# Suffix sums spread over query rows by TensorE, a reordered DMA queue, other PSUM banks for the output transposes, and loop weight tiles gathered in DRAM

## Chip, cores and metric

One core of one Trainium2 chip. The metric is the device time of one launch in microseconds (us), the median of several runs.

## What is computed

One inference step of a two-layer decoder trunk, width 1024, 16 heads of 64, all in fp32. There are 512 new prompt tokens (one sequence) and 64 sample tokens (8 sequences of 8), so 576 rows. Layer A is a gated short convolution over all rows. Its output gives one set of keys, values and log forget gates. Layer B projects queries and a SiLU gate and attends. The sample rows also attend to 2048 past rows for each sequence, kept in pages of 128 rows.

```python
q, z = jnp.split(_rmsnorm(x, g) @ w_in, 2, axis=-1)
s = jnp.einsum('nqhd,nkhd->nhqk', q, k) * (HEAD_DIM ** -0.5)
s = s + (fq - fk)                 # F: cumulative sum of the log forget values, past included
p = jax.nn.softmax(jnp.where(kpos <= qpos, s, -inf), axis=-1)
out = x + (einsum(p, v) * silu(z)) @ w_out
# k_all, v_all, F_all: cache pages named by page_table, then the new sample rows
```

For the past, fk enters as the sum of the log forget values behind a row (the suffix sum), one number for each sequence, head and past row.

## The kernel before

The kernel is written for the engines directly: each engine has its own instruction list in a fixed order, and semaphores tie them together. SyncE (SP) issues nearly all DMAs, in the order written.

Every fp32 product with a weight is made of three fp32r products (high by high, low by high, high by low). So each weight tile [128, 8, 128] is loaded raw (`w_raw`, two slots), scaled by the norm gains on GpSimd (POOL, L529 and L552), rounded to its high part on ScalarE (ACT, L630 or L681), and its low part is subtracted on VectorE (DVE) or POOL (L914, L998, L561).

The stages:

- The mixer, up to 235 us: 8 turns of 4 weight tiles, 48 matmuls each (L1294).
- The output slabs of layer A, to 300 us: 4 slabs of 256 columns, 5 row tiles each (L1320). DVE adds each tile to the residual (L993, `out_tile`), and TensorE (PE) waits for that before it reuses a bank. At their start DVE makes the suffix sums `logf_sums` (L1001), POOL stores them to DRAM as fp32, and SP waits for the stores before it loads on.
- The queries, to 385 us: 8 tiles (`query`).
- The loop `heads(i)`, eight turns, to 845 us. Turn i does two heads of the prompt and all the past of sample sequence i.
- The output slabs of layer B.

A turn of the loop, in PE's order: the tile of values is projected (`project(0)`), its last eighth after a wait for 8 of the 16 key pages. Key pages are transposed by 32 x 32 blocks on DVE (`turn_keys`, L1068). Then come the first half of the past scores (`past_scores(0)`, L1451, into the four banks T0, T1, C0, C1), the tile of keys (`project(1)`), the other half of the scores, and the z tile (`project(2)`) in pieces between other work. In DVE's and ACT's order: DVE adds the suffix sums to the scores and takes the maximum (L1099, then three tiny instructions L1104 to L1106 that give the softmax bias, semaphore `b_nbs`). ACT takes the exponential (L777, `b_es`), PE transposes the probabilities (L1264), and ACT and DVE copy them out (L747, L1081). PE then goes through 16 value pages (L1558, `b_used` frees a page's slot in `page_ring`). Between them it does four blocks of the prompt attention: `block_scores(r)`, on DVE `block_max(r)` (L1124, and the tiny L1129 and L1130), on ACT `block_exp(r)`, on DVE `block_divide(r)` (L1138), on PE `block_turn(r)`, `block_out(r)`. The next turn's key pages go into the slots as they come free.

On the side, POOL makes the next weight tiles: scale the z tile, `low_b` of it, norm the keys (`b_normed`), scale the next values tile, `low_b` of it once ACT has rounded it (`high_b(KT + 3*i + 3, 0)`), scale the next keys tile, copy the queries, `low_b` of that tile (`high_b(KT + 3*i + 4, 1)`).

Of the kernel before, what the change touches and what calls it, by code (L numbers as in the profile page):

```python
# [23 lines left out]
F32 = mybir.dt.float32  # L24
# [7 lines left out]
P = 128  # L32
# [81 lines left out]
def build(nc, ctx, x_prompt, x_sample, state_conv, cache_k, cache_v, cache_logf, page_table,  # L114
# [70 lines left out]
    LS = place("sum_past", [P, NB])  # L185
    assert at["top"] <= nc.sbuf_usable_end, at["top"]
# [11 lines left out]
    CS = place("logf_sums", [P, H, PAGE], over=at["sample_scores"])  # L198
    STN = place("state_rows", [2 * NB, D], over=at["new_keys"])
# [32 lines left out]
    def sem(name):  # L232
# [30 lines left out]
    b_turned, b_scored, b_taken = sem("k_pages_turned"), sem("past_scored"), sem("past_scores_taken")  # L263
# [49 lines left out]
    def _(sp):  # L313
# [36 lines left out]
        mixer(KT - 1, True)  # L350

# [13 lines left out]
        sp.wait_ge(s_sfx_st, 16 * NB)  # L365
# [60 lines left out]
        for m in range(KT):  # L426
            r = 32 * (m % 4) + 16 * (m // 4)
            sp.dma_start(CK[r:r + 16, :],
                         f_dram[2 * m:2 * m + 2, SEQ:TOK].unsqueeze(1).to_broadcast([2, NQ, NS])).then_inc(s_ck, 16)
        for n in range(4, KT + 3):  # L430
# [3 lines left out]
            else:  # L434
                load_w(*((wkv, D), (wkv, 0), (wqz, KT * P))[n - KT], (0, 1, 1)[n - KT])
# [11 lines left out]
        def values(pages, i, last):  # L447
# [4 lines left out]
            if not last:  # L452
                sp.wait_ge(b_split, KT + 3 * i + 1)
                load_w(wkv, (i + 1 + KT) * P, 0)

            for n in range(NPG):
# [3 lines left out]
                if n == 7 and not last:  # L460
                    sp.wait_ge(b_split, KT + 3 * i + 3)
                    load_w(wkv, (i + 1) * P, 1)
# [1218 lines left out]
```

## Time and profile before

| | us |
|---|---|
| Median of 3 runs (925.36 to 931.59) | 925.96 |
| The profiled execution, its own time | 924.18 |
| Its span (first to last instruction) | 922.4 |
| PE busy | 837.3 (91%) |
| DVE busy | 545.6 (59%) |
| ACT busy | 342.4 (37%) |
| POOL busy | 217.3 (24%) |
| Data moved by DMA | 206.39 MB |

The span and its rows belong to the one profiled execution. 1.8 us of its time lie outside of the span. Busy times of engines overlap, so what ends last has to be read from the waits. A turn is named here by S, the start of its first half of past scores: 385.6 in turn 0, 624.0 in turn 4, 681.8 in turn 5, 797.4 in turn 7, the last.

### The profile page before, as it was taken

The page shows a single profiled execution, that of the slowest core. Times are in us where ns is not written, and L with a number is a line of the kernel's source. Part 1 is how long each engine was busy: PE and PEld are TensorE (multiplying, and loading weights), DVE is VectorE, ACT ScalarE, POOL GpSimd, SP SyncE. Part 2 cuts the span into 40 slices and gives each one's busy share as a digit, 9 for nine tenths or more (in the row PEclk, how much of TensorE's full clock was granted, in tenths as well). Part 3 has the DMA queues.
Part 4 walks back from the last instruction along what each step waited for, and adds up shares of the span by engine and source line. Part 5 has one row for each costly group of instructions (what it writes and reads, how often), then busy time and mean ns, then how long its engine had stood idle before and what let it go on. Part 6 is the DMA issues. An engine that isn't in the chain of part 4 may idle for free.

```text
span 922.4 us, 22692 instructions
## 1 busy us (share of the span) xinstructions
PE 837.3 (91%) x8516; PEld 701.5 (76%) x8516; DVE 545.6 (59%) x1039; ACT 342.4 (37%) x728; POOL 217.3 (24%) x130
## 2 busy tenths in 40 slices
PE   3799999999998999698988988889888998897998
PEld 3799999999998899474765756567566675664998
DVE  4745565454436523747758578586695866946642
ACT  4333333332204444335345352452533525245210
POOL 2244333323211022213221321413223132130000
PEclk9999999999999999899999999999999999998999
DMA  7232323322554653298999999999999999994212
GB/s 212 69 88 72 91 70 89 91 68 91 140 137 122 238 178 120 71 365 267 315 370 299 376 349 318 395 317 379 366 329 397 292 381 391 312 402 140 92 46 104
DMA packets 148451, 206.39 MB, mean 224 GB/s; under 512 B 10527, under 2 KB 93136, under 8 KB 147266
## 3 DMA queue, kind: packets, MB, share of 16 engines
q1 hardware_dynamic: 138802, 199.40, 65.1%
q10 hardware_dynamic: 9088, 4.46, 1.6%
q0 software_dynamic: 528, 2.10, 0.8%
q8 instruction: 20, 0.33, 0.1%
q14 instruction: 13, 0.11, 0.0%
HBM read 195.29 MB, written 10.63 MB: 223 GB/s over the span
## 4 chain that ended last, share of the span: by engine, by line
PE 68%; DVE 14%; SPq 7%; issue 5%; DMA 4%; ACT 1%; DVEq 0%; POOL 0%; ACTq 0%; POOLq 0%
PE psum L1294 37%; PE psum L1320 10%; PE psum L1451 7%; DVE page_ring L1068 5%; SPq L387 4%; PE psum L1264 4%; PE psum L1558 3%; DMA page_ring<-in_cache_k 2%; PE psum L1491 1%; PE psum L1513 1%; DVE probs_odd L1138 1%; DMA w_raw<-in_a_w_in 1%; DMA w_raw<-in_a_w_out 1%; DVE tiny L1129 1%; DVE probs L1124 1%
## 5 line engine op out<-in xcount | busy, mean ns | idle before, releaser
L1294 PE MATMUL psum<-xn_high,w_high 128*128 128x256 f32 x992 | 226.8, 310 | 19.8 <-DVE page_ring L1068 16.9
L1294 PE MATMUL psum<-xn_low,w_high 128*128 128x256 f32 x992 | 213.6, 297 | 0.0
L1294 PE MATMUL psum<-xn_high,w_low 128*128 128x256 f32 x992 | 213.5, 297 | 0.0
L1294 PEld LDWEIGHTS psum<-xn_high,w_high 128*128 128x128 f32 x992 | 165.8, 191 | 52.8 <-issue 29.6
L1294 PEld LDWEIGHTS psum<-xn_high,w_low 128*128 128x128 f32 x992 | 168.2, 190 | 0.0
L1294 PEld LDWEIGHTS psum<-xn_low,w_high 128*128 128x128 f32 x992 | 168.1, 190 | 0.0
L1068 DVE STREAM_TRANSPOSE page_ring<-page_ring 128x1024 f32<-128x1024 f32 x128 | 149.5, 1215 | 6.2 <-DMA page_ring<-in_cache_k 5.6
L552 POOL TENSOR_TENSOR w_raw<-w_raw,gains 128x1024 f32<-128x1024 f32 x32 | 60.7, 1898 | 224.7 <-DMA w_raw<-in_b_w_in 213.4
L914 DVE TENSOR_TENSOR w_low<-w_raw,w_high 128x1024 fp32r<-128x1024 f32 x32 | 50.4, 1576 | 77.4 <-ACT w_high L630 77.4
L561 POOL TENSOR_TENSOR w_low<-w_raw,w_high 128x1024 fp32r<-128x1024 f32 x22 | 52.4, 2380 | 131.4 <-ACT w_high L681 131.4
L529 POOL TENSOR_TENSOR w_raw<-w_raw,gains 128x1024 f32<-128x1024 f32 x30 | 61.9, 2063 | 86.9 <-DMA w_raw<-in_a_w_in 86.9
L1558 PE MATMUL psum<-page_ring,p_turned 128*32 128x256 f32 x1024 | 75.6, 390 | 0.0
L1451 PE MATMUL psum<-page_ring,q_current 32*32 32x512 f32 x2048 | 73.5, 614 | 0.0
L630 ACT ACTIVATE w_high<-w_raw 128x1024 fp32r<-128x1024 f32 x32 | 33.9, 1060 | 94.1 <-PE psum L1294 66.7
L1451 PEld LDWEIGHTS psum<-page_ring,q_current 32*32 32x32 f32 x2048 | 34.2, 104 | 27.4 <-issue 18.1
L681 ACT ACTIVATE w_high<-w_raw 128x1024 fp32r<-128x1024 f32 x30 | 31.7, 1056 | 60.4 <-POOL w_raw L552 51.2
L1558 PEld LDWEIGHTS psum<-page_ring,p_turned 128*32 128x32 f32 x1024 | 23.5, 108 | 20.9 <-issue 13.7
L732 ACT ACTIVATE q_current<-queries 32x64 f32 (+1 forms) x128 | 32.5, 254 | 3.9 <-DVE queries L1045 1.0
L1081 DVE COPY probs_t<-psum 128x512 f32<-128x512 f32 (+3 forms) x32 | 15.4, 482 | 27.5 <-PE psum L1264 27.3
L1096 DVE COPY ks_t<-k_t 128x64 f32 (+1 forms) x8 | 1.6, 196 | 50.5 <-PE psum L1451 50.5
L797 ACT ACTIVATE probs<-probs,tiny 128x512 f32<-128x512 f32 (+1 forms) x32 | 19.3, 604 | 25.4 <-DVE tiny L1130 24.4
L1264 PE MATMUL psum<-constants,sample_scores 128*128 128x128 f32 x128 | 18.6, 278 | 10.6 <-DVE p_turned L1081 8.6
(243 smaller groups left out, 1431.8 us busy)
## 6 DMA issues: line engine op xcount, KB each, us to landing
page_ring<-in_cache_k SPq DMA_DIRECT2D x256, 256.0 KB, 6.2
page_ring<-in_cache_v SPq DMA_DIRECT2D x128, 512.0 KB, 9.6
w_raw<-in_a_w_in SPq DMA_DIRECT2D x32, 512.0 KB, 4.0
sample_scores<-suffix_scratch SPq DMA_DIRECT2D x8, 1024.0 KB, 12.4
w_raw<-in_b_w_in SPq DMA_DIRECT2D x16, 512.0 KB, 6.0
w_raw<-in_kv_w SPq DMA_DIRECT2D x16, 512.0 KB, 8.9
w_raw<-in_a_w_out SPq DMA_DIRECT2D x4, 1024.0 KB, 4.8
f_broad<-f_scratch SPq DMA_DIRECT2D x8, 512.0 KB, 7.6
```

The lines of the kernel that those rows point to most:

```text
L387: sp.dma_start(ring[:, n, e * HALF_D:(e + 1) * HALF_D], src.rearrange("a p n -> (a p) n")).then_inc(b_page[n], 16)
L529: pool.tensor_tensor(WR[:, q % 2, :, :], WR[:, q % 2, :, :], gain(G_A), ALU.mult).then_inc(a_scaled, 1)
L552: pool.tensor_tensor(WR[:, slot, :, :], WR[:, slot, :, :], gain(g), ALU.mult).then_inc(b_scaled, 1)
L561: pool.tensor_tensor(WL[:, slot, :, :], WR[:, slot, :, :], WH[:, slot, :, :].bitcast(F32), ALU.subtract).then_inc(b_split, 1)
L630: act.activation(WH[:, slot, :, :], WR[:, slot, :, :], ACT.Copy).then_inc(a_high, 1)
L914: dve.tensor_tensor(WL[:, slot, :, :], WR[:, slot, :, :], WH[:, slot, :, :].bitcast(F32), ALU.subtract).then_inc(a_split, 1)
L1068: dve.transpose(ring[:, n, :], ring[:, n, :]).then_inc(b_turned, 1)
L1264: return pe.transpose(out, src, CT[0:r, C_ID:C_ID + r])
L1294: mm = pe.matmul(PS[:, bank + h, 0:c.stop - c.start], w[:, k, :], x[:, k, c], start=(k == 0 and n == 0), stop=(k == KT - 1 and n == 2))
L1320: mm = pe.matmul(PS[0:r, bank, 0:SLAB], x[:, k, toks(t)], wp[:, k, :], start=(k == 0 and p == 0), stop=(k == KT - 1 and p == 2))
L1451: mm = pe.matmul(PS[32 * j:32 * j + 32, T0 + g, :].rearrange("p (n k) -> p n k", k=32), QC[32 * g:32 * g + 32, j, 64 * h + 32 * a:64 * h + ...
L1558: mm = pe.matmul(PS[32 * j:32 * j + 32, OS, 0:4 * HD].rearrange("p (a n) -> p a n", a=2), PTS[:, k, 32 * j:32 * j + 32], ring[:, k, :].rea ...
```

## The change

- The suffix sums are stored as three bf16 parts (ACT rounds, DVE subtracts, twice over). In a turn 48 rows of 4 KB are loaded instead of 128 rows of 8 KB. 16 bf16 matmuls with a 0/1 matrix `EACH` write them into the four score banks before the scores are added (`start=False`). DVE no longer adds; it takes one maximum over all four banks, and ACT takes the exponential from PSUM.
- The transposes of new keys and values go to the banks OP and OS. Those of the keys move ahead of the second half of the scores, those of the values right behind it. Four of the eight z pieces follow at once, then a wait for two of the exponentials ahead of `block_scores(0)`.
- `high_b(KT + 3*i + 3, 0)` moves on ACT from behind the probabilities' copies to just behind the values' copy, ahead of the exponentials. `high_b(KT + 3*i + 4, 1)` moves from after block 3 to between blocks 0 and 2.
- On DVE `block_divide(0)` goes ahead of `block_max(1)`, and `block_divide(3)` ahead of the first `turn_keys` of the next turn. Four key pages of turn 0 are transposed during the last two queries.
- The stores of new keys and values go from ACT's queue to SP's. SP reads 12 of 16 page numbers before the first key load, and the others behind it.
- 24 weight tiles are copied DRAM to DRAM in the mixer (rows of 512 B gathered to rows of 4 KB), and the loop loads them from there.

```diff
-    suffix_dram = nc.dram_tensor("suffix_scratch", [NB, H, PAST], F32, kind="Internal").ap()
+    suffix_dram = nc.dram_tensor("suffix_scratch", [NB, 3, H, PAST], BF16, kind="Internal").ap()
+    w_dram = nc.dram_tensor("w_scratch", [3 * KT, P, D], F32, kind="Internal").ap()
...
+        def gather_w(i, q):
+            w, col = ((wkv, i + KT), (wkv, i), (wqz, i + KT))[q]
+            sp.dma_start(w_dram[bass.ds(3 * i + q, 1), :, :].rearrange("a p (k n) -> (a p) k n", k=KT),
+                         w[:, :, bass.ds(col * P, P)]).then_inc(s_wst, 16)
...
                 load_a(i + q // 2, (q + 2) % 4)
+                if q < 3:
+                    gather_w(i, q)
...
         def load_suffix(b):
-            src = suffix_dram[bass.ds(b, 1), :, :].rearrange("a h n -> (a h) n")
-            sp.dma_start(SS[:, :], src.unsqueeze(1).to_broadcast([H, NQ, PAST])).then_inc(b_sfx, 16)
+            sp.dma_start(SUF[:, :], suffix_dram[bass.ds(b, 1), :, :, :].rearrange("a t h n -> (a t h) n")).then_inc(b_sfx, 16)
...
-            pages = [page_of(i + 1, n) for n in range(NPG)]
+            pages = [page_of(i + 1, n) for n in range(12)]
             for n in range(NPG):
                 load_keys(pages, n, (b_used, NPG * i + n + 1))
+                if n < 2:
+                    pages += [page_of(i + 1, 12 + 2 * n), page_of(i + 1, 13 + 2 * n)]
+                if n == 3:
+                    outputs(i)
...
+            if n == 1:
+                act.wait_ge(s_sfx, 1)
+                for t in range(3):
+                    if t:
+                        act.wait_ge(s_sfr, t)
+                    act.activation(CSB[t][:, :, :], CS[:, :, :], ACT.Copy).then_inc(s_sfp, 1)
...
+            turned0(KN[:, 0:QB, :], PS[:, OP, :].rearrange("p (k n) -> p k n", k=4)).then_inc(b_t0f, 1)
             act.wait_ge(b_proj, KT + 3 * i + 2)
             act.activation(prompt2(VT[:, 0:SEQ]), pr, ACT.Copy)
             act.activation(VT[:, SEQ:TOK], sa, ACT.Copy).then_inc(b_dact, 1)
...
+            turned0(VN[:, :, :], PS[:, OP, :].rearrange("p (k n) -> p k n", k=4)).then_inc(b_t0f, 1)
+            if not last:
+                high_b(KT + 3 * i + 3, 0)
             act.wait_ge(b_nbs, i + 1)
             act.wait_ge(b_lp, i)
...
+            for g in (2, 3, 0, 1):
+                ss = SS[:, :].rearrange("p (n g k) -> p n g k", g=4, k=32)[:, :, g, :]
+                act.activation(ss, PS[:, T0 + g, :].rearrange("p (n k) -> p n k", k=32), ACT.Exp,
+                               bias=TINY[:, 13:14], accum_out=TINY[:, 16 + g:17 + g]).then_inc(b_es, 1)
...
             block_turned(0)
+            if not last:
+                act.wait_ge(b_proj, KT + 3 * i + 3)
+                high_b(KT + 3 * i + 4, 1)
             block_exp(2)
...
+        for t in range(2):
+            dve.wait_ge(s_sfp, t + 1)
+            dve.tensor_tensor(CS[:, :, :], CS[:, :, :], CSB[t][:, :, :], ALU.subtract).then_inc(s_sfr, 1)
...
-            for g in range(4):
-                ss = SS[:, :].rearrange("p (n g k) -> p n g k", g=4, k=32)[:, :, g, :]
-                dve.tensor_tensor_reduce(ss, PS[:, T0 + g, :].rearrange("p (n k) -> p n k", k=32), ss,
-                                         1.0, NEG, ALU.add, ALU.max, TINY[:, 4 + g:5 + g]).then_inc(b_taken, 1)
-            dve.wait_ge(b_taken, 4 * i + 4)
...
-            ch.link(dve.tensor_reduce(TINY[:, 14:15], TINY[:, 4:8], AX, ALU.max))
+            ch.link(dve.tensor_reduce(TINY[:, 14:15], PS[:, T0:T0 + 4, :].rearrange("p a n -> p (a n)"), AX, ALU.max))
             ch.link(dve.tensor_tensor(ms, TINY[:, 14:15], cq, ALU.add))
             dve.tensor_tensor(TINY[:, 13:14], cq, ms, ALU.subtract).then_inc(b_nbs, 1)
...
+            pe.wait_ge(b_sfx, 16 * (i + 1))
+            project(0, [KT - 2])
+            for g in range(4):
+                for j in range(4):
+                    pe.matmul(PS[32 * j:32 * j + 32, T0 + g, :].rearrange("p (n k) -> p n k", k=32),
+                              EACH[:, 32 * j:32 * j + 32],
+                              SUF[:, :].rearrange("p (n g k) -> p n g k", g=4, k=32)[:, :, g, :],
+                              start=True, stop=False, tile_position=(0, 32 * j))
...
+            pe.wait_ge(b_ln, i + 1)
+            pe.wait_ge(b_normed, i + 1)
+            rows_turned(KN_T)
             pe.wait_ge(b_turned, NPG * i + NPG)
...
+            rows_turned(VT)
+            project(2, [0, 1, 2, 3])
+            pe.wait_ge(b_es, 4 * i + 2)
             pe.wait_ge(b_qt, i + 1)
             block_scores(0)
+            pe.wait_ge(b_es, 4 * i + 4)
             for g in range(4):
-                pe.wait_ge(b_es, 4 * i + g + 1)
...
+                if g in (1, 2):
+                    project(2, [3 + g])
```

## Rows read from the trace of the kernel before

**Rows 1.** Windows of turns 2 and 5: busy us, granted clock, DMA share, GB/s.

```profile
506.00:565.00 59.00, 51.70 (x654) 36.59 (x652) 40.54 (x84) 24.51 (x64) 14.70 (x8) 1.00 1.03 345
...
681.80:739.60 57.80, 52.05 (x663) 36.77 (x666) 40.63 (x84) 24.51 (x64) 14.75 (x8) 1.00 1.02 348
```

**Rows 2.** Windows of 2 us inside turn 4.

```profile
638.00:640.00 2.00, 2.00 (x79) 1.14 (x62) 0.00 (x0) 0.00 (x0) 0.74 (x1) 1.00 1.01 404
...
676.00:678.00 2.00, 2.00 (x17) 2.00 (x16) 2.00 (x3) 0.52 (x2) 0.00 (x0) 1.00 0.90 191
```

**Rows 3.** PE in turn 4, in order of time: start, us, instruction [idle before].

```profile
636.02 4.46 PE L1451 MATMUL psum<-page_ring,q_current 32*32 32x512 f32 x128
...
657.05 1.09 PE L1264 MATMUL psum<-constants,probs 128*128 128x128 f32 x8 [1.54 <-DVE probs L1138]
...
671.14 0.53 PE L1264 MATMUL psum<-constants,probs_odd 128*128 128x128 f32 x2 [1.56 <-DVE probs_odd L1138]
...
680.77 0.53 PE L1294 MATMUL psum<-xn_high,w_high 128*128 128x256 f32 x2 [1.22 <-DVE page_ring L1068]
```

**Rows 4.** POOL in the same turn.

```profile
635.46 1.43 POOL L568 TENSOR_TENSOR k_t<-k_t,rsqrt 128x576 f32<-128x576 f32 x1
...
652.06 2.39 POOL L561 TENSOR_TENSOR w_low<-w_raw,w_high 128x1024 fp32r<-128x1024 f32 x1 [13.32 <-ACT w_high L681]
654.39 1.92 POOL L552 TENSOR_TENSOR w_raw<-w_raw,gains 128x1024 f32<-128x1024 f32 x1
665.26 0.61 POOL L575 COPY q_t<-queries 128x512 f32 x1 [8.96 <-PE psum L1495]
668.65 2.35 POOL L561 TENSOR_TENSOR w_low<-w_raw,w_high 128x1024 fp32r<-128x1024 f32 x1 [2.78 <-ACT w_high L681]
```

**Rows 5.** DVE in the same turn.

```profile
640.75 0.69 DVE L1099 CUSTOM_DVE_ANT_1 sample_scores<-psum,sample_scores 128x512 f32<-128x512 f32 x1
...
643.79 0.16 DVE L1106 TENSOR_TENSOR tiny<-f_query,max_past 128x1 f32 x1
...
652.10 0.56 DVE L1124 CUSTOM_DVE_ANT_0 probs_odd<-psum,f_broad 128x384 f32<-128x384 f32 x1
...
653.27 1.19 DVE L1129 TENSOR_TENSOR tiny<-tiny 128x2 f32<-128x2 f32 x1
654.50 1.82 DVE L1130 TENSOR_TENSOR tiny<-tiny 128x2 f32<-128x2 f32 x1
...
669.12 2.16 DVE L1138 TENSOR_SCALAR probs_odd<-probs_odd,tiny 128x128 f32<-128x128 f32 x2
```

**Rows 6.** ACT in the same turn, its copy of the transposed values and the rounding moved.

```profile
645.41 0.58 ACT L747 ACTIVATE v_rows<-psum 128x512 f32<-128x512 f32 x1
...
650.92 1.06 ACT L681 ACTIVATE w_high<-w_raw 128x1024 fp32r<-128x1024 f32 x1 [1.27 <-DVE p_turned L1081]
```

**Rows 7.** PE at the start of turn 0.

```profile
383.80 0.85 PE L1294 MATMUL psum<-xn_high,w_high 128*128 128x256 f32 x2 [5.51 <-DVE page_ring L1068]
385.54 6.51 PE L1451 MATMUL psum<-page_ring,q_current 32*32 32x512 f32 x128
```

**Rows 8.** The same, ACT.

```profile
374.23 4.43 ACT L732 ACTIVATE q_current<-queries 32x64 f32<-32x64 f32 x16 [1.01 <-DVE queries L1045]
```

**Rows 9.** A window of 1 us after a PE gap of 2.4 us, layer A's end.

```profile
291.00:292.00 1.00, 1.00 (x8) 1.00 (x6) 0.89 (x4) 0.08 (x1) 0.00 (x0) 0.55 0.00 0
```

**Rows 10.** DVE at the first output slabs.

```profile
238.52 2.29 DVE L1001 TENSOR_TENSOR logf_sums<-psum,logf_sums 128x2048 f32<-128x2048 f32 x1 [0.84 <-PE psum L1337]
...
249.98 0.42 DVE L993 TENSOR_TENSOR residual<-psum,residual 64x256 f32<-64x256 f32 x1 [2.31 <-PE psum L1320]
```

**Rows 11.** DMAs by tile: KB each, us to landing (median).

```profile
sample_scores<-suffix_scratch SPq DMA_DIRECT2D x8, 1024.0 KB, 12.4
```

**Rows 12.** Mixer, a weight tile on POOL, and then on ACT.

```profile
198.93 1.99 POOL L529 TENSOR_TENSOR w_raw<-w_raw,gains 128x1024 f32<-128x1024 f32 x1 [5.33 <-DMA w_raw<-in_a_w_in]
...
203.24 1.06 ACT L630 ACTIVATE w_high<-w_raw 128x1024 fp32r<-128x1024 f32 x1 [5.34 <-PE psum L1294]
```

More of the change, by code:

```diff
@@ L185, in build @@
     LS = place("sum_past", [P, NB])
+    EACH = place("each_head", [3 * H, P], BF16)
     assert at["top"] <= nc.sbuf_usable_end, at["top"]
@@ L198, in build @@
     CS = place("logf_sums", [P, H, PAGE], over=at["sample_scores"])
+    CSB = [place(f"suffix_part{t}", [P, H, PAGE], BF16, over=o) for t, o in enumerate(
+        (at["o_past"], at["o_past"] + 2 * H * PAGE, at["new_keys"]))]
+    SUF = place("suffix", [3 * H, PAST], BF16, over=at["sample_scores"])
     STN = place("state_rows", [2 * NB, D], over=at["new_keys"])
@@ L675, in _ @@
             high_slab(1 - n % 2)
+            if n == 1:
+                act.wait_ge(s_sfx, 1)
+                for t in range(3):
+                    if t:
+                        act.wait_ge(s_sfr, t)
+                    act.activation(CSB[t][:, :, :], CS[:, :, :], ACT.Copy).then_inc(s_sfp, 1)
         act.wait_ge(s_wfs, 1)
@@ L822, in heads @@
             block_turned(2)
-            if not last:
-                high_b(KT + 3 * i + 4, 1)
             act.wait_ge(b_zm, i + 1)
@@ L1003, in _ @@
         low_slab(1, 0)
+        for t in range(2):
+            dve.wait_ge(s_sfp, t + 1)
+            dve.tensor_tensor(CS[:, :, :], CS[:, :, :], CSB[t][:, :, :], ALU.subtract).then_inc(s_sfr, 1)
+        one_head = [ident[0:3 * H, t * H:(t + 1) * H].unsqueeze(2).to_broadcast([3 * H, H, NQ]) for t in range(3)]
+        each = EACH[:, :].rearrange("p (h q) -> p h q", q=NQ)
+        dve.tensor_tensor(each, one_head[0], one_head[1], ALU.add).then_inc(s_each, 1)
+        dve.wait_ge(s_each, 1)
+        dve.tensor_tensor(each, each, one_head[2], ALU.add).then_inc(s_each, 1)
         with dve.Fori(0, NSLAB // 2 - 1) as j:
@@ L1050, in _ @@
                 query(2 * j + s, s)
+        for n in range(2):
+            turn_keys(0, n)
         query(KT - 2, 0)
@@ L1055, in _ @@
         dve.tensor_copy(FQN[:, :, :], PS[:, T0, 128:128 + QB * H].rearrange("p (t h) -> p t h", h=H)).then_inc(s_fnr, 1)
+        for n in range(2, 4):
+            turn_keys(0, n)
         query(KT - 1, 1)
@@ L1063, in _ @@
         done_b = ch.n
-        def turn_keys(b, n):
-            dve.wait_ge(b_page[n], 48 * b + 32)
-            dve.transpose(ring[:, n, :], ring[:, n, :]).then_inc(b_turned, 1)
-        for n in range(4):
-            turn_keys(0, n)
         def heads(i, last):
@@ L1163, in heads @@
             block_turned(2)
+            block_divide(3)
             if not last:
                 turn_keys(i + 1, 0)
-            block_divide(3)
-            if not last:
-                turn_keys(i + 1, 1)
             block_turned(3)
@@ L1173, in heads @@
             if not last:
-                turn_keys(i + 1, 2)
-                turn_keys(i + 1, 3)
+                for n in range(1, 4):
+                    turn_keys(i + 1, n)
             assert t1[0] == 8
@@ L1454, in past_scores @@
                                     half[32 * g:32 * g + 32, :, c:c + 32],
-                                    start=(h == 0 and a == 0), stop=(h == 3 and a == 1), tile_position=(32 * g, 32 * j))
+                                    start=False, stop=(h == 3 and a == 1), tile_position=(32 * g, 32 * j))
                 mm.then_inc(b_scored, 1)
@@ L1476, in heads, with rows_turned @@
             project(1, range(1, KT - 1))
+            def rows_turned(src):
+                for t in range(QB):
+                    mm = turn(PS[:, OP, t * P:(t + 1) * P], src[:, toks(t)])
+                mm.then_inc(b_t0, 1)
+                turn(PS[0:NS, OS, 0:P], src[:, SEQ:TOK]).then_inc(b_t1, 1)
+                t0[0] += 1
+                t1[0] += 1
+            pe.wait_ge(b_ln, i + 1)
+            pe.wait_ge(b_normed, i + 1)
+            rows_turned(KN_T)
             pe.wait_ge(b_turned, NPG * i + NPG)
```

92 lines of the change are left out of this document (42 added, 50 removed).

## Prediction

> **What bounds the kernel now.** I read the windows of the loop's turns first. A middle turn takes 57.8 us with PE busy 52.05, and the DMA share is at 1.02 all the time; an earlier turn takes 59.0 [rows 1]. So two things are close to their limit. Then the engines inside one turn. PE stands idle before `block_turn(0)` (1.54 us), `block_turn(3)` (1.56) and the last eighth of the values' projection (1.22) [rows 3]. The first two are DVE's: its `tiny` instructions L1129 and L1130, 128 x 2 numbers, take 1.19 and 1.82 us and end at 654.46 and 656.32, each at the end of a POOL instruction (654.45 and 656.31), and L1138 (two instructions, 2.16) ends 0.28 after POOL's L561 at 671.00 [rows 4, 5]. So a DVE instruction with two inputs in SBUF waits for the whole of a POOL instruction under way, and for the next if that follows at once. L1124, which reads PSUM and one SBUF tile, started in the same POOL instruction and took only 0.56 [rows 4, 5]. This is the view on which the forecast turns.
>
> **DMA.** The suffix load moves 1 MB and lands after 12.4 us [rows 11]; a window behind its issue moved 191 GB/s, where pages move at 404 [rows 2]. At 191 to 404 it holds the DMA engines for 5.5 to 2.6 us a turn, and 192 KB for 0.5 to 1.0. With the larger weight rows, which I bound from 0 to the same halving (1.6 MB at 191 or 404: 0 to 4.3 us), DMA gives back 1.6 to 9.3 us a turn, and I take 5. A turn of 57.8 at share 1.02 would then need about 53. So DMA is no longer late, and what a turn costs is set by the engines' chain. The early turns lose their 1.2 us of excess.
>
> **The chain of a turn, after S.** Before, the second half of the scores starts at 636.02 and takes 4.46, so it ends at 640.48, S + 16.5 [rows 3]. The keys' transposes now lie ahead of it: 0.7 us, once `b_normed` is there. That came at 636.89 [rows 4], S + 12.9, after a late z tile; with DMA freed, and the tile's load issued when it is, I take it to be in time at S + 11.3. Bounds: 0 to 1.6 us. The scores end at E = S + 17.2.
>
> Then DVE. The bias `b_nbs` was ready at 643.95, 3.5 us after the scores [rows 5]. Now there is one reduction over 2048 columns. L1099 takes 0.69 for 512 of which 0.15 are fixed by its follower's start, so 2048 take 4 x 0.53 + 0.16 = 2.3. It starts 0.27 after E as L1099 does [rows 5] and ends at E + 2.55; L1105 would start at E + 2.7 and L1106 end at E + 3.0.
>
> But ACT and POOL. The values' transposes now follow the scores at once (0.7 us), ACT copies them (0.58, its next instruction 0.48 behind its start), and directly behind it comes `high_b(KT + 3*i + 3, 0)`, 1.06 us [rows 6]. It ends at E + 0.7 + 0.5 + 1.06 = E + 2.3. POOL's L561 starts 0.08 behind such a rounding (650.92 + 1.06 to 652.06) and takes 2.39 [rows 4, 6]. So POOL holds from E + 2.35 to E + 4.75, and L1105, which comes at E + 2.7, waits. POOL's L552 followed L561 with no gap and takes 1.92 [rows 4], so it holds to E + 6.6, and L1106 ends at E + 6.65. This is exactly the pair that now delays L1129 and L1130; the change moves it in front of the bias, on which everything on PE hangs. `b_nbs`: S + 23.9 instead of S + 19.9.
>
> The Trainium skill, SBUF — State Buffer, section Who interferes with whom, states the same lock and adds that "issue order, not op shape, decides who blocks". By that rule L1105 would go free if it issued before E + 2.35, and the result would be that of the first rival. The trace agrees with the lock; no row shows the opposite order.
>
> PE does the values' transposes and four z pieces (0.8 each) to E + 4.2 and waits for two exponentials, about E + 8.4: four idle microseconds. From the bias to the end of `block_scores(1)` I count as before: exponentials 1.5, `block_scores(0)` 1.3, transposes and z pieces, the wait for DVE's copy, 8.0 in all, against 7.9 before. It ends at S + 31.9, before at 651.8, S + 27.8.
>
> Then the gains. The z piece of k = 4 is done already (0.85), and the idle 1.54 ahead of `block_turn(0)` goes, since `block_divide(0)` stands first and POOL is quiet by then: `block_turn(0)` starts at S + 35.2; before at 657.05 [rows 3], S + 33.0, with 0.85 still to do. Net +1.3.
>
> **The end of a turn.** `high_b(KT + 3*i + 4, 1)` is early, so L561 follows the queries' copy at 665.87 instead of 668.65 [rows 4]. It no longer meets L1138 (2.16) [rows 5] but L1129 of block 3, which comes at the same moment, for 2.4 us. PE waits 0.8 instead of 1.56 for `block_turn(3)`. DVE's row of work to the eighth transposed page is the limit there (PE idle 1.22 for it) [rows 3]; it gets 0.4 longer. The 16 bf16 matmuls fall into that idle time. No row has them. The 128 instructions of a score half run sixteen at a time, so one such set of 512 columns takes 4.46 / 8 = 0.56 us [rows 3]. The new ones can run four at a time at most: 4 x 0.56 = 2.2 us at that pace, 16 x 0.56 = 9 if they don't overlap. I take half of the first, 1.0, since they are bf16 and single, and about 1.4 fit ahead of the wait; so they cost 0 (bounds 0 and 7 a turn, the latter only without overlap, for which the rows of sixteen speak against). A turn: 57.8 + 1.3 + 0.4 = 59.5.
>
> The stores on SP's queue wait for copies long made, and SP's fewer page reads start the key loads up to 2 us earlier; both lie beside the chain: 0. If that cover is gone, key loads are late by under 1 us.
>
> **PE's clock.** After a gap of 5.51 us the same scores took 6.51 instead of 4.46, and after one of 2.4 us the granted clock was 0.55 in the window behind it; after gaps of 1.5 us it stayed at 1.00 [rows 1, 3, 7, 9]. 0.5 is 1.2 GHz. A gap of four microseconds lies among those with a fall. The cost is 0 to 2 us a turn (2.05 is the row's excess); part hides in the wait for the other exponentials. I take 0.4 on average.
>
> **Outside.** Turn 0: four transposes are done in idle time of DVE during the last queries. The wait of 5.51 us for the eighth page shrinks by four pages; but the wait for `q_current`, ended at 378.66 [rows 8], now stands ahead of an eighth and the 16 matmuls: 378.7 + 0.8 + 1.0 + 1.1 = 381.6 in place of 385.6, that is -4.0. The scores run at the full clock again, in turn 0's own length. Output slabs: DVE's two subtractions (2.3 each, as L1001) and ACT's three roundings (2 x 1.06 less one fixed part, 2.0 each [rows 6]) alternate from 240.8 [rows 10]; the second subtraction ends at 240.8 + 2 x 2.0 + 2 x 2.3 = 249.4 at the latest, and only then DVE adds the first tiles, which were added as PE made them, the fifth at 249.98 [rows 10]. PE needs four additions (0.42 each) before the second slab, so at about 251.5 and not 249.7: +1.8 (bounds 0 and 3). Mixer: an added 512 KB copy behind each of 24 loads. POOL was done with a tile at 200.92 and ACT took it up at 203.24, when PE freed the slot [rows 12]. So landing may slip 2.3 us with nothing lost, and the copy stands behind the load: 0, bounds 0 and 5 in all. The last turn has no POOL work for a next tile: -0.7.
>
> **Sum.** Turn 0's scores start at 385.6 - 4.0 + 1.8 = 383.4 (S of turn 7 was 797.4, 411.8 later). Seven turns of 59.5 + 0.4 are 419.3; the rest, 125.0 - 0.7, is 124.3. Span 927.0 instead of 922.4: +4.6. On the execution's own 924.18 that is 928.8, and on the median 925.96, which lies 1.8 above that execution, 930.6. 1% is about what a measurement of this kernel can tell from no change.
>
> **Rivals.**
> 1. The bias goes free of POOL. For it: the margin is 0.35 us of a chain of three estimates. Against: each of them has a row, and none is off by more than 0.1. Then `b_nbs` is at S + 20.2, PE idle 0.5 instead of four us; `block_turn(0)` starts at S + 31.4. A turn is 55.8. 383.4 + 7 x 55.8 + 124.3 = 898.3, -24.1, the median 902. This also holds if the z pieces, DMA and DVE orders give more than I count.
> 2. Slower: the clock falls in each turn, in the gap ahead of `block_scores(0)`. It decides as soon as the gap reaches that of the rows with a fall (2.4 us). 2 us a turn: 7 x 61.5 = 430.5, span 938.2, median 942. For it: two gaps of two fell. Against: PE waits there anyway.
> 3. The change doesn't do what it says: DMA stays the limit, since the saturated share was 1.02 with PE's waits elsewhere. Then turns stay at 57.8 at most: 383.4 + 404.6 + 124.3 = 912.3, median 916. Against: in turn 5 no wait of the chain is a DMA's.
>
> **Chances.** Forecast 0.38 (920 to 936), first rival 0.29 (895 to 910), second 0.21 (936 to 945), third 0.12. Faster by over 1% (below 916.7): rivals 1 and most of 3, 0.37. Slower by over 1% (above 935.2): rival 2 and the forecast's edge, 0.24. Within 1%: 0.39. The range, 8 in 10, reaches over both signs: 898 to 942. The forecast's own is 920 to 936.
>
> **What would show it.** L1105 and L1106 long (about 2 us each) and ending with POOL's L561 and L552; PE idle three to four microseconds ahead of `block_scores(0)`, with ACT's exponentials as releaser; no idle time ahead of `block_turn(0)`; granted clock under 1.00 in the turns; a DMA share clearly under 1 in the loop; the first scores near 382 and at 4.4 us; PE idle about 1.8 us at 250. The prediction is wrong if the tiny instructions before the bias take 0.16 us each, or if the mixer shows PE waiting for weights.

## The result, and the profile after

The changed kernel takes 938.37 us (median of 4 runs, 936.22 to 940.1), the kernel before on the same chip 925.66. The ratio is 1.013, with a 95% interval of 1.010 to 1.017: slower by 1.3%. The forecast was 930.6, with its own band from 920 to 936 and a range of 898 to 942. So the time lies in the range, but outside the forecast's band: it is near the time that the second rival had given (942, a span of 938.2), which had a chance of 0.21.

The head of the page of the changed kernel, with its lines for the granted clock and for DMA (40 slices):

```profile
span 938.3 us, 22981 instructions
PE 855.9 (91%) x8644; PEld 719.2 (77%) x8644; DVE 548.8 (58%) x979; ACT 346.5 (37%) x731; POOL 231.0 (25%) x146
PEclk8799999999999999989989899899898998998999
DMA  7445544544545553579969979699697996995212
```

DMA is no longer at 9 all through the loop, and the granted clock dips in the loop, where it was even before. The windows of turns 2 and 4, then of 1 us stretches in turn 4. The columns are us, busy us of PE, PEld, DVE, ACT and POOL (instructions), granted clock, DMA share, GB/s:

```profile
507.40:568.96 61.56, 55.16 (x672) 39.33 (x671) 41.26 (x76) 24.24 (x64) 14.74 (x8) 0.94 0.89 323
630.30:691.70 61.40, 55.14 (x671) 39.52 (x670) 41.26 (x76) 24.25 (x64) 14.76 (x8) 0.94 0.89 319
653.00:654.00 1.00, 0.00 (x0) 0.00 (x0) 1.00 (x2) 0.05 (x1) 0.91 (x1) 1.00 1.02 406
654.00:655.00 1.00, 0.00 (x0) 0.00 (x0) 0.12 (x1) 1.00 (x3) 0.00 (x0) 0.93 1.03 410
655.00:656.00 1.00, 0.55 (x2) 0.50 (x4) 0.00 (x0) 1.00 (x5) 0.00 (x0) 0.50 0.98 393
660.00:661.00 1.00, 1.00 (x6) 0.98 (x5) 0.58 (x1) 0.00 (x0) 0.00 (x0) 0.50 0.25 98
661.00:662.00 1.00, 1.00 (x8) 1.00 (x7) 0.00 (x0) 0.13 (x1) 0.00 (x0) 0.66 0.00 0
662.00:663.00 1.00, 1.00 (x9) 0.84 (x7) 0.00 (x0) 1.00 (x3) 0.00 (x0) 1.00 0.00 0
```

Each of the seven turns takes 61.4 to 61.6 us. Before, turns 1 to 6 take 57.8 to 59.6 and turn 0 takes 61.6, a mean of 58.8; the 59.0 of [rows 1] is a window inside turn 2, which is 59.6 long. PE is busy 55.1 us and not 52, mainly because the granted clock is 0.50, which is 1.2 GHz, for some 7 us of each turn; 1.04 us are the new bf16 matmuls. PE in turn 4, all with an idle time over 0.5 us and both halves of the scores (columns as in [rows 3]):

```profile
630.33 4.46 PE L1488 MATMUL psum<-page_ring,q_current 32*32 32x512 f32 x128
642.96 4.46 PE L1488 MATMUL psum<-page_ring,q_current 32*32 32x512 f32 x128
655.45 1.65 PE L1550 MATMUL psum<-k_t,q_t 64*128 64x384 f32 x4 [4.15 <-ACT sample_scores L821]
679.53 0.66 PE L1572 MATMUL psum<-probs_t,v_rows 128*64 128x128 f32 x8 [1.23 <-ACT probs_t L790]
690.75 0.54 PE L1331 MATMUL psum<-xn_high,w_high 128*128 128x256 f32 x2 [0.89 <-DVE page_ring L1087]
```

So S, the start of the first half of the scores, is 630.33, and E, the end of the second, is 647.42. The gap ahead of `block_scores(0)` (L1550) is 4.15 us. What it waits for (rows of DVE, then ACT, then POOL):

```profile
647.77 2.28 DVE L1146 TENSOR_REDUCE tiny<-psum 128x1 f32<-128x2048 f32 x1
650.20 1.86 DVE L1147 TENSOR_TENSOR max_past<-tiny,f_query 128x1 f32 x1
652.10 1.82 DVE L1148 TENSOR_TENSOR tiny<-f_query,max_past 128x1 f32 x1
...
648.54 1.05 ACT L724 ACTIVATE w_high<-w_raw 128x1024 fp32r<-128x1024 f32 x1
653.95 0.69 ACT L821 ACTIVATE sample_scores<-psum,tiny 128x512 f32<-128x512 f32 x1 [4.37 <-DVE tiny L1148]
...
649.66 2.39 POOL L597 TENSOR_TENSOR w_low<-w_raw,w_high 128x1024 fp32r<-128x1024 f32 x1 [6.57 <-ACT w_high L724]
652.01 1.90 POOL L588 TENSOR_TENSOR w_raw<-w_raw,gains 128x1024 f32<-128x1024 f32 x1
675.15 0.61 POOL L611 COPY q_t<-queries 128x512 f32 x1 [21.24 <-PE psum L1554]
675.72 2.37 POOL L597 TENSOR_TENSOR w_low<-w_raw,w_high 128x1024 fp32r<-128x1024 f32 x1
```

Read it from the ends. L1147 ends at 652.06, 0.01 after POOL's L597; L1148 ends at 653.92, 0.01 after L588. Two instructions on 128 numbers take 3.68 us. They hold the bias `b_nbs`, that holds ACT's first exponential, and that holds PE. This is called the lock below: a DVE instruction with two tiles in SBUF as inputs stands still until the POOL instruction under way has ended, as these two do. Turn 7 has no next weight tile for POOL, and there the same two take 0.16 us each and PE's gap is 0.46.

Where the 15.9 us by which the span is longer (938.3 against 922.4) arose: turn 0's scores begin at 384.57 (385.6 before), seven turns take 430.0 (411.8 before), the rest 123.7 (125.0). So 18.2 us were lost in the loop, 2.6 a turn, and 2.3 gained outside.

### The profile page after: what moved, and what is told of

Its sections match the earlier page's. It is cut to its first block, busy times and chain, and to the rows that moved or that the text cites. A ratio compares the mean times of both kernels' runs of the same rounds, so it can differ in the third digit from the quotient of the medians.

```text
span 938.3 us, 22981 instructions
## 1 busy us (share of the span) xinstructions
PE 855.9 (91%) x8644; PEld 719.2 (77%) x8644; DVE 548.8 (58%) x979; ACT 346.5 (37%) x731; POOL 231.0 (25%) x146
## 4 chain that ended last, share of the span: by engine, by line
PE 74%; DVE 16%; ACT 3%; issue 2%; DMA 2%; SPq 1%; DVEq 0%; POOL 0%; ACTq 0%; POOLq 0%
PE psum L1331 37%; PE psum L1357 10%; PE psum L1488 8%; PE psum L1301 6%; PE psum L1612 5%; DVE page_ring L1087 5%; PE psum L1550 2%; DVE tiny L1146 2%; PE psum L1572 2%; DVE tiny L1168 2%; DVE max_past L1147 1%; DVE tiny L1148 1%; DMA w_raw<-in_a_w_in 1%; PE psum L1552 1%; DMA w_raw<-in_a_w_out 1%
## 5 line engine op out<-in xcount | busy, mean ns | idle before, releaser
L1331 PE MATMUL psum<-xn_high,w_high 128*128 128x256 f32 x992 | 230.1, 314 | 8.9 <-DVE page_ring L1087 5.6
L1331 PE MATMUL psum<-xn_low,w_high 128*128 128x256 f32 x992 | 216.0, 300 | 0.0
L1331 PEld LDWEIGHTS psum<-xn_high,w_high 128*128 128x128 f32 x992 | 168.9, 194 | 37.3 <-issue 24.2
L1331 PEld LDWEIGHTS psum<-xn_low,w_high 128*128 128x128 f32 x992 | 170.4, 193 | 0.0
L588 POOL TENSOR_TENSOR w_raw<-w_raw,gains 128x1024 f32<-128x1024 f32 x32 | 60.7, 1899 | 207.0 <-DMA w_raw<-w_scratch 132.8
L950 DVE TENSOR_TENSOR w_low<-w_raw,w_high 128x1024 fp32r<-128x1024 f32 x32 | 44.3, 1385 | 83.8 <-ACT w_high L666 83.8
L564 POOL TENSOR_TENSOR w_raw<-w_raw,gains 128x1024 f32<-128x1024 f32 x30 | 65.5, 2185 | 82.5 <-DMA w_raw<-in_a_w_in 82.5
L597 POOL TENSOR_TENSOR w_low<-w_raw,w_high 128x1024 fp32r<-128x1024 f32 x22 | 52.6, 2392 | 63.8 <-ACT w_high L724 63.8
L1550 PE MATMUL psum<-k_t,q_t 64*128 64x384 f32 (+2 forms) x96 | 22.0, 542 | 29.5 <-ACT sample_scores L821 29.5
L611 POOL COPY q_t<-queries 128x512 f32 x7 | 4.3, 611 | 148.5 <-PE psum L1554 148.5
L1550 PEld LDWEIGHTS psum<-k_t,q_t 64*128 64x128 f32 x96 | 8.7, 220 | 36.0 <-ACT sample_scores L821 31.3
L821 ACT ACTIVATE sample_scores<-psum,tiny 128x512 f32<-128x512 f32 x32 | 21.6, 686 | 32.2 <-DVE tiny L1148 32.2
```

Source lines behind the costliest of these rows:

```text
L564: pool.tensor_tensor(WR[:, q % 2, :, :], WR[:, q % 2, :, :], gain(G_A), ALU.mult).then_inc(a_scaled, 1)
L588: pool.tensor_tensor(WR[:, slot, :, :], WR[:, slot, :, :], gain(g), ALU.mult).then_inc(b_scaled, 1)
L597: pool.tensor_tensor(WL[:, slot, :, :], WR[:, slot, :, :], WH[:, slot, :, :].bitcast(F32), ALU.subtract).then_inc(b_split, 1)
L950: dve.tensor_tensor(WL[:, slot, :, :], WR[:, slot, :, :], WH[:, slot, :, :].bitcast(F32), ALU.subtract).then_inc(a_split, 1)
L1331: mm = pe.matmul(PS[:, bank + h, 0:c.stop - c.start], w[:, k, :], x[:, k, c], start=(k == 0 and n == 0), stop=(k == KT - 1 and n == 2))
L1550: pe.matmul(PS[:, bank, 0:w - P], QT[pr, toks(s)], KN_T[pr, 0:w - P], start=True, stop=True)
```

## The experiments

Most start from the changed kernel or from the first experiment; where one starts from another kernel, it says so. All ratios are to the kernel before on the same chip; medians come from different chips, on which the kernel before has 924.6 to 928.9. Four kernels first ask whether the lock of POOL on the bias is the cause, against a rival: that the new order of PE's and the DMA's work is slow by itself.

**Rounding early.** The ACT rounding that starts POOL goes ahead of the values' copy, so that POOL's first instruction is done when the bias comes.

```diff
+            if not last:
+                high_b(KT + 3 * i + 3, 0)
             turned0(VN[:, :, :], PS[:, OP, :].rearrange("p (k n) -> p k n", k=4)).then_inc(b_t0f, 1)
-            if not last:
-                high_b(KT + 3 * i + 3, 0)
```

> The changed kernel with one line moved on ACT: the rounding of the next values tile goes ahead of the copy of the transposed values, right behind the copies of the value projection. Theory (POOL's port work meets the two tiny DVE instructions that make the bias): POOL's low part and scaling then run about 3 to 7 us before the second half of the scores ends (E - 2.3 to E + 2), L1147 and L1148 take 0.16 us each, the PE gap of 4.15 us before block_scores(0) shrinks to 0.5, the granted clock stays at 1.00, a turn takes 55.8 us instead of 61.4, and the median is near 938 - 7 x 5.6 = 899. Rival (the turn is long because of the new order of banks and transposes, or the DMAs): the gap and the time stay, 935 to 940.

Measured: 902.16 us, ratio 0.973 (0.968 to 0.979). DVE, then POOL, in turn 4 of this kernel:

```profile
628.58 0.16 DVE L1147 TENSOR_TENSOR max_past<-tiny,f_query 128x1 f32 x1
628.78 0.16 DVE L1148 TENSOR_TENSOR tiny<-f_query,max_past 128x1 f32 x1
...
623.18 2.38 POOL L597 TENSOR_TENSOR w_low<-w_raw,w_high 128x1024 fp32r<-128x1024 f32 x1 [1.60 <-ACT w_high L724]
629.74 1.90 POOL L588 TENSOR_TENSOR w_raw<-w_raw,gains 128x1024 f32<-128x1024 f32 x1 [4.19 <-DMA w_raw<-w_scratch]
```

The same two instructions take 0.16 each, PE's gap is 0.78, turns 1 to 4 are 55.4 to 56.1 us (forecast 55.8). One moved instruction turns a loss of 1.3% into a gain of 2.7%. The margin is thin: L588 waits for its tile and starts 0.80 us after L1148 has ended. In turn 0 the tile is there sooner, L588 starts at 402.13 and L1147, at 402.45, takes 1.59, with a gap of 2.21 on PE.

**Rounding late.** The same, moved behind ACT's two copies of turned sample scores.

```diff
             turned0(VN[:, :, :], PS[:, OP, :].rearrange("p (k n) -> p k n", k=4)).then_inc(b_t0f, 1)
-            if not last:
-                high_b(KT + 3 * i + 3, 0)
...
             for g in (0, 2):
                 turned0(PTS[:, 4 * g:4 * g + 4, :], PS[:, T0, :].rearrange("p (k n) -> p k n", k=4)).then_inc(b_t0f, 1)
+            if not last:
+                high_b(KT + 3 * i + 3, 0)
```

> The changed kernel with the same rounding moved back to where the kernel before had it, behind the exponentials and the two copies of transposed probabilities. Theory: the bias goes free (L1147, L1148 at 0.16 us), the gap before block_scores(0) is 0.5 us and the clock stays, but POOL's pair now meets L1168 and L1169 of block 1 or the divisions, as before the change: a turn of about 57.5 us, median near 911. Rival (order of banks, DMAs): 935 to 940.

Measured: 905.46 us, 0.979 (0.973 to 0.985). The lock is then met by a division, two instructions on 128 x 512:

```profile
636.68 3.14 DVE L1177 TENSOR_SCALAR probs<-probs,tiny 128x512 f32<-128x512 f32 x2
```

It takes 0.88 when free. The time is below the 911 that was expected, and turns 1 to 6 take 56.2 to 57.0 us and not 57.5. On PE a wait of 0.67 us for ACT stands ahead of `block_out(0)`, where "rounding early" has none.

**Gap filled.** The lock stays; PE does 30 matmuls of no use in the gap, which keep it busy.

```diff
+            pe.wait_ge(b_t0f, 8 * i + 2)
+            for k in range(30):
+                pe.matmul(PS[:, OP, 0:HALF], WH[:, 1, k % KT, :], XH[:, k % KT, 0:HALF], start=True, stop=True)
             pe.wait_ge(b_es, 4 * i + 2)
```

> The changed kernel with 30 useless matmuls of 256 columns (3.6 us) in the gap ahead of block_scores(0); their result is overwritten. It prices the clock alone. Theory (the gap lets the clock fall for 6.8 us, and that costs about 2 us a turn on top of the late bias): granted clock 1.00 in the turns, a turn of 59.5 us instead of 61.4, median near 925. Rival (the clock's fall is hidden by the waits for the exponentials): under 0.5 us a turn, 935 to 940.

Measured: 922.9 us, 0.995 (0.992 to 0.999). PE in turn 4, and the second of DVE's two instructions in the same turn:

```profile
638.56 3.76 PE L1585 MATMUL psum<-xn_high,w_high 128*128 128x256 f32 x30
642.89 0.92 PE L1550 MATMUL psum<-k_t,q_t 64*128 64x384 f32 x4 [0.57 <-ACT sample_scores L821]
652.49 1.09 PE L1301 MATMUL psum<-constants,probs 128*128 128x128 f32 x8
...
639.53 1.82 DVE L1148 TENSOR_TENSOR tiny<-f_query,max_past 128x1 f32 x1
```

The bias is as late as in the changed kernel (L1148 1.82; `block_scores(0)` at S + 25.15, there S + 25.12), but L1550 takes 0.92 and not 1.65, and `block_turn(0)` starts at S + 34.75 where the changed kernel's is at 667.78, S + 37.45. A turn is 58.7 us. So of the loss, 2.7 us a turn is the fall of the clock alone, and the lock without it 2.9 (58.7 against the 55.8 of "rounding early").

**Bias by one input.** The bias is minus the maximum of the past, which doesn't need `max_past`: it is made by a TENSOR_SCALAR with one tile as input, and the two-input sum comes after it.

```diff
+            dve.tensor_scalar(TINY[:, 13:14], TINY[:, 14:15], -1.0, None, ALU.mult).then_inc(b_nbs, 1)
             ch.link(dve.tensor_tensor(ms, TINY[:, 14:15], cq, ALU.add))
-            dve.tensor_tensor(TINY[:, 13:14], cq, ms, ALU.subtract).then_inc(b_nbs, 1)
```

> The changed kernel with the bias made as minus the maximum by one TENSOR_SCALAR with a single SBUF input, ahead of the addition for max_past. It tells whether the lock needs two SBUF inputs. If a tiny TENSOR_SCALAR goes free beside POOL: it takes 0.15 us, the bias is ready at E + 2.9, a turn takes about 55.8 to 56 us, median near 900. If it waits for POOL like the others: it ends with POOL's L597 at E + 4.8, 1.9 us sooner than now since the second wait is off the path, gap near 2.3 us, turn 57.5 to 59.5, median 912 to 925. If the theory of the lock is wrong altogether: 935 to 940.

Measured: 903.34 us, 0.974 (0.968 to 0.979). DVE and POOL:

```profile
629.67 0.15 DVE L1147 TENSOR_SCALAR tiny<-tiny 128x1 f32<-128x1 f32 x1
629.80 1.86 DVE L1148 TENSOR_TENSOR max_past<-tiny,f_query 128x1 f32 x1
...
629.25 2.39 POOL L597 TENSOR_TENSOR w_low<-w_raw,w_high 128x1024 fp32r<-128x1024 f32 x1 [6.49 <-ACT w_high L724]
```

POOL's instruction began before both. The one-input one went through in 0.15, the two-input one behind it waited 1.86, off the path; so it goes in turns 0 to 6. That settles it: PE's new order and the DMA's work are the same in this kernel and in the changed one, and the rival falls.

**Both.** The two cures together.

> Both cures at once: the bias by one input, and the rounding of the next weight tile ahead of the values' copy. Theory (the lock was the whole loss, and either cure takes it away whole): nothing is left for the second to win, so 902 +- 3 us, the ratio of each alone (0.9732 and 0.9736); L1147 and L1148 at 0.16 each, PE's gap ahead of the first scores of the block at 0.5 to 0.8. Rival (each cure removes only half, the rest being POOL's hold on other DVE instructions): another 4 to 8 us less, 894 to 898.

Measured: 903.27 us, 0.974 (0.970 to 0.978), the same as either. The lock on the bias was the whole of what these cures can win.

The next four start from "rounding early" and ask for the other terms of the sum.

**Second tile late.** `high_b(KT + 3 * i + 4, 1)` goes back behind `block_turned(2)`.

> On top of the first tile's early rounding, the second tile's rounding goes back to where the kernel before had it, behind ACT's third copy of turned probabilities. The prediction gave its early place 0.8 us a turn (PE's wait ahead of the third block_turn 0.8 and not 1.56), so by it this kernel takes 7 x 0.8 = 5.6 us more than the 902.2 of the first: 908; POOL's L597 would end on DVE's division L1177, which then takes about 2 us in block 3. Rival: the place is worth nothing, because DVE's row of work up to the eighth turned page is the limit there: 902 to 903, with PE's waits of 1.22 (L1572) and 0.9 (L1331) only changing places.

Measured: 904.77 us, 0.977 (0.971 to 0.983): no difference that can be told from "rounding early". But the waits of PE changed places (us in all, times, longest; the first two rows of "rounding early", the last of this kernel):

```profile
PE psum L1572 <- ACT probs_t L790: 8.6, 7, 1.2
PE psum L1331 <- DMA suffix<-suffix_scratch: 3.3, 4, 1.5
```

```profile
PE psum L1330 <- DMA suffix<-suffix_scratch: 12.5, 7, 3.2
```

The wait of 1.2 us a turn (L1572, it is `block_out(2)` that waits) went: DVE's two-input instruction of block 3 (L1168, 2.27 in the changed kernel, 0.16 here), on which ACT's `block_exp(3)` and behind it `block_turned(2)` wait, is free again. What it gave was lost to the suffix, for which PE now waits in every turn; behind the waits of 3.19, 2.10 and 1.63 us the scores take 6.10, 5.15 and 5.34 us and not 4.46, while behind one of 1.70 they take 4.46.

**Suffix early.** The suffix load is issued behind the fourth key page and not behind the ninth.

```diff
                 if n == 3:
-                    outputs(i)
-                if n == 8:
-
                     sp.wait_ge(b_t0, 8 * i + 4)
                     sp.wait_ge(b_t1, 8 * i + 4)
                     load_suffix(i + 1)
+                    outputs(i)
```

> On top of the first tile's early rounding, the suffix load is issued behind the fourth key page and not behind the ninth, some 8 us earlier. With the lock gone, PE waited for the suffix in three turns of seven (2.7 us in all, up to 1.5) and for the page at the same place in four (2.7 in all). If DMA is late only at that load: 2 to 3 us less than 902.2, 899 to 900, and no wait for the suffix. Rival: the DMA queues are full (share 0.97), so that an earlier suffix makes the pages behind it late by what it takes itself: 902 or 903, with the waits on L1087 in place of the suffix.

Measured: 903.14 us, 0.972 (0.965 to 0.978), no difference from "rounding early" that its spread can show (898.2 to 914.85). No row of it stands here; that PE waits for the turned page once the suffix is early is read from "second late, suffix early" below.

**No gather.** The copies in DRAM are left out, and the tiles are loaded from the inputs.

```diff
-                if q < 3:
-                    gather_w(i, q)
...
-            sp.dma_start(WR[:, slot, :, :].rearrange("p k n -> p (k n)"),
-                         w_dram[bass.ds(3 * i + q, 1), :, :].rearrange("a p n -> (a p) n")).then_inc(b_raw[slot], 16)
+            w, col = ((wkv, i + KT), (wkv, i), (wqz, i + KT))[q]
+            load_w(w, col * P, slot)
```

> On top of the first tile's early rounding, no copy of the weights in DRAM: the loop's tiles are loaded from the inputs as in the kernel before, in short rows, and the mixer issues no copies. Turns of 55.7 us had a DMA share of 0.97 with the long rows. Theory (the long rows free 0 to 4.3 us of DMA a turn, as the prediction bounded it; I take 2.5): the share is then above 1 and DMA is late, turns of 57 to 58 us, 902.2 + 7 x 1.8 = 915, from 908 to 920, with PE's waits on the suffix, on pages, or POOL's on w_raw; the mixer is no faster. Rival (the long rows are worth nothing in the loop): 902, and less by up to 5 if the copies slowed the mixer.

Measured: 905.11 us, 0.976 (0.972 to 0.980). It is not 915, and within the noise of "rounding early". In the window 440 to 790 this kernel has a DMA share of 1.01; "rounding early" has 0.98. DMA issues by tile (KB each, us to landing), this kernel's two and then the gathered one of "rounding early". The first mixes 8 tiles of the loop with the 8 of the queries (4.1 us by themselves in "rounding early"); the second is the loop's alone:

```profile
w_raw<-in_b_w_in SPq DMA_DIRECT2D x16, 512.0 KB, 5.8
w_raw<-in_kv_w SPq DMA_DIRECT2D x16, 512.0 KB, 8.9
```

```profile
w_raw<-w_scratch SPq DMA_DIRECT2D x24, 512.0 KB, 9.8
```

**Second late, suffix early.** The edits of those two together.

> The first tile's rounding early, the second tile's late, and the suffix load behind the fourth key page. With the second tile late, PE no longer waited ahead of the last block_out (1.22 a turn before), but waited 12.5 us in seven turns for the suffix, so that nothing was won (904.8). With the suffix early the wait went to the eighth turned page instead (0.9 a turn), under the second tile early. If the two waits were each other's cover, taking both away gives 7 x 1.2 to 1.8 us: 890 to 894. Rival: DVE's row of work up to the eighth page, or the full DMA queues, is the real limit; then PE waits there for longer, for pages, and the time stays at 900 to 905.

Measured: 894.4 us, 0.968 (0.964 to 0.973). The median is 7.8 us under that of "rounding early", on another chip; by the ratios it is 0.5%, with intervals that overlap. The profiled executions tell the two apart: seven turns take 382.4 us here, 393.0 in "rounding early" and 395.5 in "second late". So one edit alone gave nothing and the other nothing that shows, but both together some 10 us of the loop: the two waits were each other's cover. PE's waits of this kernel:

```profile
PE psum L1328 <- DVE page_ring L1084: 6.4, 7, 0.9
PE psum L1547 <- ACT sample_scores L819: 5.9, 8, 0.8
```

The suffix and `block_out(2)` are gone from the list. Four turns from 383.55 to 602.46 are 54.7 us each, at a DMA share of 0.98.

**Keys late.** On "rounding early", the four key pages of turn 0 are turned behind the queries as before.

> On top of the first tile's early rounding (902.2), the four key pages of turn 0 are turned where the kernel before had them, behind the queries. The prediction counted the whole move of turn 0 at -4.0 us: by it PE waits again some 4 to 5.5 us for the eighth page ahead of the first scores, which then run at 1.2 GHz and take 6.5 and not 4.46. So 3 to 6 us more: 905 to 908, S of turn 0 at 386 to 388. Rival: the wait for q_current (1.6) covers it, and the gain at S was something else: 902.

Measured: 905.39 us, 0.978 (0.974 to 0.983). PE at the start of turn 0:

```profile
384.89 0.84 PE L1328 MATMUL psum<-xn_high,w_high 128*128 128x256 f32 x2 [2.69 <-DVE page_ring L1087]
386.63 6.15 PE L1485 MATMUL psum<-page_ring,q_current 32*32 32x512 f32 x128
```

S is 386.63 and not 382.58, and the first scores run at the lower clock again (4.46 when not), as was expected.

**Before, with the gather.** The kernel before with this part of the change alone.

> The kernel before with the gather alone: copies in DRAM during the mixer and 4 KB rows in the loop, and the 1 MB suffix load, ACT's and DVE's work as they were. The prediction gave the long rows 0 to 4.3 us of DMA in a turn, where the share was 1.02. On top of the changed kernel their absence cost nothing measurable (905.1 against 902.2), and the loads landed no sooner. Theory now (row size is worth nothing here): within 0.5% of before, 922 to 930. Rival (DMA is the limit of the kernel before, and long rows give it back 1 us a turn or more): 915 to 920, with turns under 57.8.

Measured: 922.1 us, 0.996 (0.993 to 0.999): a gain of 0.4%, at the edge of what the theory allowed and short of the rival. The DMA share in 440 to 790 is 1.00; before, 1.03.

**Page earlier.** Starting from "second late, suffix early", DVE turns the next turn's first key page before `block_turned(1)` and the second before `block_turned(3)`.

```diff
             block_divide(1)
+            if not last:
+                turn_keys(i + 1, 0)
             block_turned(1)
...
             if not last:
-                turn_keys(i + 1, 0)
+                turn_keys(i + 1, 1)
             block_turned(3)
```

> The best so far (894.4), with DVE turning the next turn's first key page before the second block's turned probabilities and its second page before the fourth block's. In every turn of that kernel PE waits 0.92 us for the eighth turned page, 6.4 in all. DVE idled 1.04 us before the second block's copy (640.85) and 0.36 before the fourth's, and one turning costs 1.2 us. If DVE's row of work is what the eighth page waits for, it ends about 1.0 us earlier, the 0.92 go down to 0 to 0.2, and the time is 888 to 890. Rival: DMA is the limit (share 0.97 and above with the turns now at 54.6 us), the page or the suffix lands no sooner, and PE waits as long for a page or for the suffix: 893 to 896.

Measured: 895.77 us (889.8 to 906.88), 0.963 (0.958 to 0.967). The wait for the page is gone, and another stands in its place:

```profile
PE psum L1300 <- POOL k_t L602: 9.1, 7, 2.7
PE psum L1330 <- DVE page_ring L1084: 0.2, 1, 0.2
```

L602 is the keys' norm on POOL, which comes behind the scaling of a weight tile that has landed late. The time is the rival's (893 to 896), and the DMA share in 440 to 790 is 0.97, against 0.98 in "second late, suffix early"; that the transfers are the limit fits this, but no run takes load off them to show it. Five turns take 53.8 to 54.5 us. The other two, with waits of 2.73 and 1.91 us for L602, take 60.4 and 59.4, since the scores behind run at the lower clock (5.74 and 4.96 us). Whether this kernel or the one that it starts from is the better one stays open, the medians lie 1.4 us apart on two chips; both beat the two kernels of this case.

## Why the prediction was right and wrong

**The lock: right.** L1147 and L1148 (L1105 and L1106 in the prediction) were forecast to end with POOL's L597 and L588 (L561 and L552) and the gap to be 4.2; they do, and it is 4.15 in each of turns 0 to 6. `b_nbs` comes at S + 23.6 (S + 23.9 forecast). "Rounding early" and "bias by one input" show that this and nothing else takes the gain. The margin of 0.35 us that carried the first rival had its sign right: POOL began 0.54 ahead of L1147. The Trainium skill, SBUF — State Buffer, section Who interferes with whom, says that issue order decides. The trace agrees: L597 started before L1147, and L588, at 652.01, 0.09 before L1148, which had to wait for the end of L1147, whose output it reads. No run shows the opposite order. Had the first rival come true, 902 was its time, and 902.16 was measured where the lock was taken away.

**The clock: the step that failed.** The prediction's sum had 0.4 us a turn, between bounds of 0 and 2, on the ground that "part hides in the wait for the other exponentials". The gap-filled kernel puts it at 2.7. The gap was known to be among those with a fall [rows 7, 9]; what was wrong was to weight the slow stretch by what might hide. From 655.45 to 661.7 PE did `block_scores(0)`, transposes and z pieces back to back at half speed. Nothing hid: all four exponentials were done at 656.7, before `block_scores(0)` ended, and PE has no idle time over 0.5 us from 655.45 on until the gap of 1.23 us that ends at 679.53. The second rival took the full excess of [rows 7], 2.05, and gave 61.5 for a turn; 61.4 was measured. Its mechanism is the right one, but that its number fits so well is luck: its price for the clock was 0.65 too small, and its chain, the forecast's 59.5, was 0.8 too long. That the time lies in the range is owed to the range's width, which held the first and the second rival as well.

**The rest of the turn: 0.8 too long.** Without the fall a turn is 58.7 and not 59.5: `block_turn(0)` starts at S + 34.75 (forecast 35.2), and from there to the next S it is 0.35 shorter. The prediction's 8.0 from the bias to the end of `block_scores(1)` carried a wait for DVE's copy. In the gap-filled kernel PE doesn't wait there, and the block ends at S + 31.1 (31.9). E is at S + 17.1 (17.2), with the keys' transposes no longer late. The early place of the second tile, which had been given 0.8 us over the old one, is worth nothing or is a loss: it moves the lock from the division (L1138 before) to L1168 of block 3 (2.27, forecast 2.4), and PE waits 1.23 there, ahead of `block_out(2)` and not of `block_turn(3)`. The 16 bf16 matmuls take 1.04 us, as assumed, and hide ahead of the page: the wait behind them is 0.89.

**DMA: right.** The share is 0.89 of 61.4, or 54.6 us of transfers in a turn, against 1.03 of some 58 before: 5 us given back, which was the value taken. The long rows' part, bounded by 0 and 4.3, is about 1.7 of it, by two pairs of kernels: 1.01 to 0.98, and 1.03 to 1.00. The rest is put down to the smaller suffix, which no run has alone. My expectation of 915 without the gather was wrong: at a share of 1.01 the seven turns took 394.0 us, against 393.0.

**Outside: right.** PE's stall at the slabs was 1.78 (1.8):

```profile
253.22 0.36 PE L1357 MATMUL psum<-w_high,gated_high 128*128 128x256 f32 x1 [1.78 <-DVE residual L1029]
```

From PE's first slab instruction (234.96 before, 236.46 after) to the scores of turn 0 it is 150.6 us before and 148.1 after, so -2.5, forecast -2.2. The 1.5 us by which the first is later is the spread of the start: other executions of kernels with the same code there have it anywhere from 233.5 to 237.0. "Keys late" has 1.8 more in that stretch than "rounding early", and 1.7 more in the scores themselves, which run at the lower clock. The mixer paid nothing that PE shows for the 24 copies: without them PE's first slab instruction came no earlier (235.58 against 234.71). The rest after turn 7's scores was 123.7 (124.3).

Together: 7 turns 430.0 against 419.3 is +10.7, S of turn 0 +1.2, the rest -0.6, which is the 11.3 between the span of 938.3 and the forecast's 927.0. The step that failed is the clock's 0.4 a turn. The gap-filled kernel gives 2.7 in its place, which is 16 us more in seven turns, less 6 for the chain that was 0.8 too long.

## What to carry to other kernels

When an instruction is moved, follow what it starts on the other engines, and look at what stands beside it there: a rounding on ACT started two POOL instructions that held up DVE's two-input instructions, and this stood ahead of a value on which PE waits. It cost more than all the rest of the change won. Price a long gap of PE twice, once as idle time and once for the work behind it at the lower clock, and take nothing off unless a row shows PE idle there. And where two edits each give nothing, look whether PE's wait changed its releaser: two waits that cover each other have to go together.

## What was not expected of the hardware

- In each gap of 4.15 us PE's granted clock fell to 0.50 just before PE started again (0.93 in the us from 654, 0.50 from 655), and it stayed there until about 661.7 with PE hardly idle; with 30 useless matmuls in the gap the mean clock of the whole run was 0.994 and not 0.958.
- A TENSOR_SCALAR of 128 x 1, with its one input and its output in SBUF, issued 0.42 us into a POOL TENSOR_TENSOR and took 0.15 us; a TENSOR_SCALAR of 128 x 512, which also takes its factor from a tile (`probs<-probs,tiny`), was held (3.14 for two, 0.88 when free). Size alone doesn't decide: eight STREAM_TRANSPOSEs of 128 x 1024 with one input took 9.12 us from 692.71 on, 1.14 each, though POOL's L588 and L597 ran from 695.58 and 698.65. Whether it is the second tile or the kind of instruction that holds the division is open.
- With two POOL instructions back to back, DVE's waiting instruction ended with the first (1.86 us), and DVE's next one, which needs its result, started 0.09 us after POOL's second and ended with that (1.82 us). So two tiny instructions in a row pay for two whole POOL instructions.
- Rows of 4 KB landed no sooner than the short ones (9.8 us against 8.9 for the tiles that only the loop loads), yet took about 1.7 us less of the DMA engines' time in a turn.
